# Attention of a head pair: both heads block by block, score products in pieces of 256 columns, value products alternating between the heads

## The reference, cut to what matters

```
p  = x @ w_in                                   # q, k, v of mixers A and B, gates
yA = attention over own chunk (64) + 8 previous chunks, learned relative bias, 16 heads of 64
yB = attention over own chunk + 2 previous chunks, ALiBi bias, sink per head, 16 q heads, 2 kv heads
s  = (q . k) / 8 + bias;  m = max(s) (B: and the sink);  p = exp(s - m)
o  = (p / sum(p)) . v                            # B: sum(p) + exp(sink - m)
h  = LN(alpha x + (sigmoid(gA) (yA wA) + sigmoid(gB) (yB wB)) w_out);  y = LN(alpha h + PEER(h))
```

## Time and profile before

| | |
|---|---|
| median of 3 runs | 4470.74 us |
| span of the profiled execution, first to last instruction | 4456.8 us |
| TensorE busy in the span | 4282.4 us, 96% |
| VectorE, ScalarE, GpSimd busy | 64%, 31%, 60% |
| share of TensorE in the chain that ended last | 66% |
| attention loops | from about 499.5 us to 1317 us of the span |
[...]

### The profile page before, as it was taken

How to read it: one execution, slowest core, us unless ns; L and a number is a source line. 1 busy time by engine, 2 the same in 40 slices (tenths; PEclk the granted TensorE clock), 3 DMA queues, 4 the chain that set the end, 5 groups by cost and what they waited for, 6 DMA issues and landing times.

```text
span 4456.8 us, 71381 instructions
## 1 busy us (share of the span) xinstructions
PE 4282.4 (96%) x26508; PEld 4120.7 (92%) x26508; DVE 2839.1 (64%) x4233; ACT 1376.0 (31%) x2750; POOL 2672.1 (60%) x1665
## 2 busy tenths in 40 slices
PE   8999999999989999799899999999999999999998
PEld 8999888878879999699899999999999999999997
DVE  1000133444442231699997899898997988988988
ACT  1000122222221110311386434343443443443444
POOL 5444322222324545244776778778887888888884
PEclk9999999999999999999999999999999999999999
DMA  5222233222233323112489999999999999999995
GB/s 202 99 102 98 96 119 128 104 81 81 78 119 122 116 90 99 38 66 76 145 276 320 382 376 398 374 372 409 416 405 377 412 418 411 417 411 416 418 418 241
DMA packets 269138, 1083.82 MB, mean 243 GB/s; under 512 B 24560, under 2 KB 90224, under 8 KB 185328
## 3 DMA queue, kind: packets, MB, share of 16 engines
q0 software_dynamic: 74736, 544.24, 29.8%
q1 hardware_dynamic: 89568, 391.16, 23.6%
q10 hardware_dynamic: 104736, 147.39, 9.7%
HBM read 1020.44 MB, written 67.63 MB: 244 GB/s over the span
## 4 chain that ended last, share of the span: by engine, by line
PE 66%; DVE 18%; DMA 6%; issue 5%; POOL 3%; ACT 1%; ACTq 0%; DVEq 0%; POOLq 0%
PE banks L497 30%; PE banks L741 15%; PE banks L675 11%; DVE work L1499 3%; DVE work L1462 2%; DVE banks L1465 2%; POOL w_lo L383 2%; PE banks L729 2%; DMA work<-in_u_rows,idx_all 2%; PE banks L566 2%; PE banks L528 2%; DMA work<-in_v_rows,idx_all 1%; POOL work L411 1%; PE banks L536 1%; DVE work L1371 1%
## 5 line engine op out<-in xcount | busy, mean ns | idle before, releaser
L383 POOL TENSOR_TENSOR w_lo<-w_raw,w_hi 128x1024 fp32r<-128x1024 f32 x472 | 1140.7, 2417 | 243.5 <-ACT w_hi L1057 229.6
L389 POOL TENSOR_SCALAR w_hi<-w_raw 128x2048 fp32r<-128x2048 f32 x134 | 289.6, 2161 | 1326.8 <-PE banks L497 1252.3
L497 PE MATMUL banks<-mv_hi,w_hi 128*128 128x256 f32 x3648 | 863.2, 318 | 62.9 <-DVE mv_lo L1203 35.4
L497 PE MATMUL banks<-mv_lo,w_hi 128*128 128x256 f32 x3648 | 835.8, 310 | 0.0
L497 PE MATMUL banks<-mv_hi,w_lo 128*128 128x256 f32 x3648 | 835.3, 310 | 0.0
L497 PEld LDWEIGHTS banks<-mv_hi,w_hi 128*128 128x128 f32 x3648 | 652.1, 189 | 127.1 <-issue 85.9
L741 PE MATMUL banks<-mv_hi,w_hi 128*128 128x384 f32 x2048 | 693.2, 338 | 43.5 <-ACT part_t L1116 22.1
L393 POOL TENSOR_TENSOR w_lo<-w_raw,w_hi 128x512 fp32r<-128x512 f32 x536 | 721.0, 1377 | 11.2
L675 PE MATMUL banks<-mv_hi,w_hi 128*128 128x384 f32 x2048 | 694.0, 339 | 4.6 <-ACTq L1083 2.0
L741 PE MATMUL banks<-mv_lo,w_hi 128*128 128x384 f32 x2048 | 690.3, 337 | 0.0
L741 PE MATMUL banks<-mv_hi,w_lo 128*128 128x384 f32 x2048 | 690.3, 337 | 0.0
(11 more groups left out here) (166 smaller groups left out, 5319.5 us busy)
## 6 DMA issues: line engine op xcount, KB each, us to landing
w_raw<-in_wstream SPq DMA_DIRECT2D x472, 512.0 KB, 7.9
w_raw<-in_wstream SPq DMA_DIRECT2D x134, 1024.0 KB, 4.8
gate_matrix<-work ACTq DMA_DIRECT2D x12, 2048.0 KB, 9.0
work<-gate_matrix ACTq DMA_DIRECT2D x32, 768.0 KB, 9.0
out_p<-work ACTq DMA_DIRECT2D x34, 320.0 KB, 2.2
work<-out_p ACTq DMA_DIRECT2D x34, 320.0 KB, 3.4
gate_scratch<-work ACTq DMA_DIRECT2D x32, 320.0 KB, 2.2
work<-gate_scratch ACTq DMA_DIRECT2D x16, 640.0 KB, 4.0
```

What stands on the lines that cost most here:

```text
L383: pool.tensor_tensor(w_lo[s][:, part], raw[s][:, part], w_hi[s][:, part].bitcast(f32), ALU.subtract) \
L389: pool.tensor_scalar(w_hi[s][:, :], raw[s][:, :], 1.0, 0.0, ALU.mult, ALU.add).then_inc(hi_done, 1)
L497: last = pe.matmul(acc(dst, h), a[s][:, P * k:P * k + P], b[h][:, k, :], start=(k == k_first and n == 0), stop=(k == k_last and n == 2))
```

## The change

The steps of a pair are reordered: block by block, both heads of a block in one round. `HEADS` becomes (head 0, head 1) of block 0, of block 1, and so on, then the sample; rounds u run over 5 blocks (`NU`) instead of 10 steps. In a round, TensorE computes the scores of both heads (alternating between them, in pieces of at most 256 columns), then k steps, the transposes of the two heads of the block before with k steps between, and the values of both heads of the block two rounds before, alternating between the heads. The buffers for scores, transposed scores, maxima and sums become four (`t % 4`, in `work2` and a wider `small`). VectorE does soft_in of both heads, then soft_out of both heads of the block before, then out_take. Score and output banks stay as they are.

```diff
-        s_sb = [area(5920, 512), area(6432, 512)]
-        pt_sb = [area(6944, 512), area(7456, 512)]
+        s_sb = [area(5920, 512), area(6432, 512), W2[:, 2048:2560], W2[:, 2560:3072]]
+        pt_sb = [area(6944, 512), area(7456, 512), W2[:, 3072:3584], W2[:, 3584:4096]]
...
-        HEADS = [(hh, i) for hh in range(2) for i in range(4)] + [(0, "sample"), (1, "sample")]
+        HEADS = [(hh, i) for i in (0, 1, 2, 3, "sample") for hh in range(2)]
         NS = len(HEADS)
+        NU = NS // 2
...
+            def scores(mix, j, u):
+                i = HEADS[2 * u][1]
+                if u:
+                    pe.wait_ge(s_taken, 1 + STEP_BASE[mix] + NS * j + 2 * u)
...
                 if i == "sample":
                     pe.wait_ge(t_taken, 1 + t_use(mix, j, ("c", 0), 1))
+                    for hh in range(2):
+                        pe.transpose(s_bank[hh][:, 0:P], st_sb[hh][:, :], ident)
+                    at, span, pieces = P, slice(0, P), ((0, P),)
                 else:
+                    w, end = width(mix, i), P * (i + 2)
+                    at, span = 0, slice(end - P, end)
+                    pieces = [(c, min(c + 2 * P, w)) for c in range(0, w, 2 * P)]
+                for lo, hi in pieces:
+                    for hh in range(2):
+                        rows = slice(HD * hh, HD * hh + HD)
+                        first = span.stop - pieces[-1][1] if i != "sample" else 0
+                        last = pe.matmul(s_bank[hh][:, at + lo:at + hi], q_t[rows, span], k_t[rows, first + lo:first + hi],
+                                         start=True, stop=True)
+                        if hi == pieces[-1][1]:
+                            last.then_inc(s_full, 1)
...
+            def values(mix, j, u):
+                i = HEADS[2 * u][1]
+                pe.wait_ge(t_taken, 1 + t_use(mix, j, ("t", 2 * u + 1), 1))
+                pe.wait_ge(o_taken, 1 + STEP_BASE[mix] + NS * j + 2 * u)
...
                     nk = width(mix, i) // P
                     for c in range(nk):
                         kb = i + 2 - nk + c
+                        for o, at, pt in parts:
+                            last = pe.matmul(o, v_nat[:, P * kb + at:P * kb + at + HD], pt[:, P * c:P * c + P],
+                                             start=(c == 0), stop=(c == nk - 1))
+                            if c == nk - 1:
+                                last.then_inc(o_full, 1)
...
-                for t in range(NS + 2):
-                    if t < NS:
-                        scores(mix, j, t)
-                    before = {0: 0, 1: 1, 6: 1, 7: 1} if mix == "a" else {0: 1, 6: 1, 7: 1, NS: 3}
-                    gemm(before.get(t, 2))
-                    if 1 <= t <= NS:
-                        transpose_p(mix, j, t - 1)
-                    if t >= 2:
-                        values(mix, j, t - 2)
-                    if t == 6:
-                        gemm(2)
+                for u in range(NU + 2):
+                    if u < NU:
+                        scores(mix, j, u)
+                    spread = ((1, 0, 0), (2, 1, 1), (1, 1, 1), (1, 1, 1), (1, 1, 1), (2, 1, 0), (2, 0, 0)) if mix == "a" else \
+                        ((2, 0, 0), (2, 1, 1), (1, 1, 1), (1, 1, 1), (2, 1, 1), (2, 1, 1), (2, 0, 0))
+                    early, between, late = spread[u]
+                    gemm(early)
+                    if 1 <= u <= NU:
+                        transpose_p(mix, j, 2 * u - 2)
+                        gemm(between)
+                        transpose_p(mix, j, 2 * u - 1)
+                        gemm(late)
+                    if u >= 2:
+                        values(mix, j, u - 2)
+                    if u == 3:
                         cached_scores(mix, j)
+                gemm(len(k_steps))
...
+                for u in range(NU + 1):
+                    if u < NU:
+                        exponents(2 * u)
+                        exponents(2 * u + 1)
+                    if u:
+                        take(mix, j, ("t", 2 * u - 2))
+                        take(mix, j, ("t", 2 * u - 1))
+                    if u == 3:
                         take(mix, j, ("c", 0))
-                    if t == 6:
                         gate_evacuate(2 * pair, 0, pair)
...
-                    for t in range(NS + 2):
-                        if 1 <= t <= NS:
-                            soft_out(mix, j, t - 1)
-                        if t < NS:
-                            soft_in(mix, j, t)
-                        if t >= 2:
-                            out_take(mix, j, t - 2, j + (PAIRS if mix == "b" else 0))
+                    for u in range(NU + 2):
+                        for t in (2 * u, 2 * u + 1):
+                            if u < NU:
+                                soft_in(mix, j, t)
+                        for t in (2 * u - 2, 2 * u - 1):
+                            if 1 <= u <= NU:
+                                soft_out(mix, j, t)
+                        for t in (2 * u - 4, 2 * u - 3):
+                            if u >= 2:
+                                out_take(mix, j, t, j + (PAIRS if mix == "b" else 0))
```

More of the change, by code:

```diff
@@ L188, in build @@
         mx = [small[:, s:s + 1] for s in range(2)]
-        nmax = [small[:, 2 + s:3 + s] for s in range(2)]
-        rsum = [small[:, 4 + s:5 + s] for s in range(2)]
-        esink = [small[:, 6 + s:7 + s] for s in range(2)]
+        nmax = [small[:, 16 + s:17 + s] for s in range(4)]
+        rsum = [small[:, 20 + s:21 + s] for s in range(4)]
+        esink = [small[:, 24 + s:25 + s] for s in range(4)]
         rden = [small[:, 8 + s:9 + s] for s in range(2)]
@@ L512, in _ @@
                     unit(s, U_QKV + 2 * i + s, (qkv_evac, 2 * i + s + 1), 0)
[L515 to L520, removed]
+            def scores(mix, j, u):
+                i = HEADS[2 * u][1]
+                if u:
+                    pe.wait_ge(s_taken, 1 + STEP_BASE[mix] + NS * j + 2 * u)
+                else:
+                    pe.wait_ge(s_taken, 1 + STEP_BASE[mix] + NS * j)
                 if i == "sample":
                     pe.wait_ge(t_taken, 1 + t_use(mix, j, ("c", 0), 1))
-                    pe.transpose(bank[:, 0:P], st_sb[hh][:, :], ident)
-                    last = pe.matmul(bank[:, P:2 * P], q_t[rows, 0:P], k_t[rows, 0:P], start=True, stop=True)
-                else:
[L526 to L529, removed]
+                    for hh in range(2):
+                        pe.transpose(s_bank[hh][:, 0:P], st_sb[hh][:, :], ident)
+                    at, span, pieces = P, slice(0, P), ((0, P),)
+                else:
+                    w, end = width(mix, i), P * (i + 2)
[9 more added lines that the diff above has]
+                            last.then_inc(s_full, 1)
             def transpose_p(mix, j, t):
@@ L535, in transpose_p @@
                 for c in range(w // P):
-                    last = pe.transpose(t_bank[:, P * c:P * c + P], s_sb[t % 2][:, P * c:P * c + P], ident)
+                    last = pe.transpose(t_bank[:, P * c:P * c + P], s_sb[t % 4][:, P * c:P * c + P], ident)
                 last.then_inc(t_full, 1)
@@ L546, in cached_scores @@
                 last.then_inc(t_full, 1)
[L548 to L553, removed]
+            def values(mix, j, u):
+                i = HEADS[2 * u][1]
+                pe.wait_ge(t_taken, 1 + t_use(mix, j, ("t", 2 * u + 1), 1))
+                pe.wait_ge(o_taken, 1 + STEP_BASE[mix] + NS * j + 2 * u)
+                v_nat = vn if mix == "a" else vn_b
+                parts = [(o_bank[HD * hh:HD * hh + HD, 0:P], HD * hh, pt_sb[(2 * u + hh) % 4]) for hh in range(2)]
                 if i == "sample":
@@ L557, in values @@
                         c = DEC_T * b
[L558 to L561, removed]
+                        for o, at, pt in parts:
+                            pe.matmul(o[:, c:c + DEC_T], cv_t[:, P * b + at:P * b + at + HD],
+                                      pt[:, c:c + DEC_T], start=(b == 0), stop=False)
+                    for o, at, pt in parts:
+                        pe.matmul(o, v_nat[:, at:at + HD], pt[:, P:2 * P], start=False, stop=True).then_inc(o_full, 1)
                 else:
```

50 lines of the change are left out of this document (22 added, 28 removed).

## The result

The changed kernel takes 4518.58 us (median of 4 runs, 4514.69 to 4522.01) against 4470.73 for the kernel before: the ratio is 1.0106, 95% interval 1.0092 to 1.012. It is slower by 48 us; forecast were 69, with a range for the whole of 4510 to 4565 us. The profiled execution has a span of 4520.2 us, 1.8 less than its time of 4522.01; so of the 13.9 us that the prediction puts between span and median before, most is the distance of that execution from the median. The forecast doesn't change by that: it is the median and 69.

What follows compares the result with a forecast made beforehand. TensorE was taken to bound the 16 attention pairs. Eight A pairs at +4.3 us and eight B pairs at +4.7 gave 72, less 3: 69 us over 4470.7, so 4540 us; forecast's own range 4510 to 4565.

Steps and rivals of the forecast that it cites:

- The waits: TensorE at transposes behind both heads' softmax chain: 7.4 us per A pair, 7.35 per B, plus 0.6 for the cached-scores copy.
- the split's inflation: VectorE's normalisation running slower beside GpSimd's split, now on TensorE's path: 0.9 us per B pair.
- The 1.0 us for the split in A pairs: GpSimd's split slowing VectorE's normalisation on TensorE's path in each A pair; bounds 0 and 1.7 us.
- The pairing: Both heads' score and value products partly overlapping on TensorE: 4.4 us saved per A pair, 3.3 per B pair.
- 2n+1 record times instead of 4n: TensorE time for both heads' n products each, near full overlap; 0.1075 us per value block, 0.21 per 256 score columns.
- series: No overlap of the heads' products on TensorE, only entries saved; taken for 128-column scores; as a rival 4568 us, chance 0.13.
- one entry's worth: The sample step on TensorE saves one group entry each for scores and values, 0.36 us per pair together.
- The half of everything: Full overlap, half of all TensorE score and value time saved: 5.75 us per A pair, 4.6 per B; total 4519.
- A rival at 0.05: TensorE's clock falls because of four gaps of 2 to 2.6 us in a pair; chance 0.05.
- the GEMM steps between the gaps: The prediction's argument against TensorE's clock falling: GEMM steps stand between the waits of a pair.
- The 3 us of gain from the later gate evacuation: Two GEMM steps behind the last values delay the second gate evacuation and ScalarE's loads; bounds 0 and 10 us.

Runs made afterwards that it cites:

- e1: The changed kernel with VectorE doing soft_out of block u-1 before soft_in of block u: 4507.64 us, 1.0074 of the kernel before.
- e2: The changed kernel with VectorE's soft_out before soft_in, and ScalarE copying block u-1's transposes in turn with block u's exponentials: 4381.81 us, 0.9796 of the kernel before.
- e8: The changed kernel with a round's GEMM steps ahead of the first transpose in rounds 2 to 4 (in B's round 1, three of four): 4448.37 us, 0.9949 of before.
- e7: The kernel before, without pairing, with VectorE doing soft_in of step t before soft_out of step t-1: 4577.46 us, 1.0232 of the kernel before.
- e5: e2 with the cached products and their copy in round 2, and VectorE taking block u-3's outputs between soft_out and soft_in: 4325.69 us, 0.9683 of before.
- e3_fill: The changed kernel with extra, never read 256-column products put into TensorE's waits ahead of the first transposes: 4481.63 us, 1.0021 of the kernel before.
- e11: e5 with one GEMM step between head 0's and head 1's part of every score and value group: 4494.27 us, 1.0052 of the kernel before.
- e6: e2 with one GEMM step between head 0's and head 1's part of every score and value group: 4537.43 us, 1.014 of the kernel before.
- e10: e5 with whole score products up to 512 columns and head 1's value products behind all of head 0's: 4336.15 us, 0.9712 of the kernel before.

## Why the prediction was right, and where it was not

**The waits: right in place and mechanism, too large in sum.** Forecast 0.47, 2.04, 2.57, 0.62 and 2.34 us in an A pair, found 0.27, 1.88, 2.43, 0.47 and 2.13. In B u=2 and u=3 came as worked out, the split's inflation included (2.01 and 3.09); u=4 gave 0.45 instead of 2.00, because the GEMM steps ahead of it ran at the lower clock: in the two B pairs where they ran at the higher one it is 1.79 and 1.81, in the other six 0.28 to 0.45. The 1.0 us for the split in A pairs was not found: in the pair above the normalisation that it slows is head 1's (1.18 us at 803.04, beside the split from 801.51 to 806.59), and a GEMM step covers that. Idle time grew by 99 us; forecast were 16 pairs of about 8.3, 133. e1, e2 and e8 show that these waits are the order of the lists: changed on VectorE and ScalarE they go, and with the GEMM steps in their place those at the first transposes shrink from 106 to 36 us. e7 shows that the order alone, on the old kernel, is worse than the whole change.

**The pairing: mis-sized by half.** The step "I count a group of n products per head at 2n+1 record times instead of 4n" failed. Both heads take as long as one, 128-column scores (0.42 us, 792.63 to 793.05; one head 0.42, 837.99 to 838.41 before) and the sample's 16-column values too (1.30 us), which the forecast had counted as series or at one entry's worth. The sample's values alone give 1.30 us a pair instead of 0.15. No run shows the 2n+1: in the trace after, the records of both heads' scores of 256 columns start in twos, one of each head, at 794.12 and 794.13 and again at 794.44 and 794.45, and one head's two before start as far apart, at 841.62 and 841.94. The reason given, that the heads share neither rows, columns nor output partitions, holds for neither kind: their score products (64*128 in the rows) share columns and output partitions, their value products (128*64) the rows, and it was enough to be apart in the other (0.63 us for both heads' scores of 256 columns, 1.03 for their values of four blocks). Saved in the loops, at full clock, are 763 - 648 = 115 us, and 763 - 640 = 123 in e5, where 62 were forecast. The half of everything, the prediction's other end, is the better estimate of this term, 83; it leaves the sample's products out as well. That it gives 4519 for the whole is chance, since it leaves out the clock.

**The clock: a rival at 0.05 that came true in part.** It takes 58 us more than before: 31 stretches at the lower level in the loops, 140 us together, against one of 10 us before. One fall as the earlier trace rows show it, 3 us at 0.50, loses 1.5 us, and three in each of the 16 pairs would lose 72, near the 58; the chance given to it was not. The argument against it, the GEMM steps between the gaps, does not hold: e3_fill shows that the gaps matter (0.98 instead of 0.92 when they are filled), and e11 that listed gaps aren't needed (0.93 in the 50 us from 710, with TensorE listed busy for 49.62).

**The sum.** +99 for idle time, -115 for the pairing and +58 for the clock are the 43 us of the loops, to 1 us. The forecast of +69 was made of +130 and -62, with nothing for the clock. So the waits were 31 us too large, and the pairing 53 too small, which the 58 of the clock covered. That the sum was near is in good part luck: with the pairing sized rightly and the clock still left out, the same working gives about 15 us more than before instead of 69, and with the measured waits too 16 less. The 3 us of gain from the later gate evacuation no run shows; they are less than the spread of the part behind the loops.

## What to carry to other kernels

When steps are merged into pairs, write down for every engine what now stands between the end of a product and the operation that hands it back: what was one head's chain became two, and with VectorE's list alone reordered (e1) TensorE's waits for its normalisation went from 106.4 us to 13.0, while 75.9 for ScalarE's copies came in their place. Put the instruction that releases the bounding engine first on every list that it passes through; changed on one list alone (e1) it gained 11 us, on both 137. The two heads' products, on disjoint halves of the array, gained by being neighbours: a GEMM step between them cost some 125 us (e6, e11), giving up the alternation about 6 (e10).

## What the runs showed of the hardware

- fp32 products of two heads on rows 0 to 63 and 64 to 127, or with outputs on columns 0 to 63 and 64 to 127, take as long as those of one head: 0.63 us for 256 columns (one head 0.63), 1.03 for four blocks (1.01), 1.30 for the sample's values (1.30).
- This holds for products that stand head behind head in the list, up to two blocks per head (0.67 us against 0.66); with three and four the overlap is partial (1.07 against 0.80 to the start of the next row, and 1.58 against 1.09 to the end of the last).
- With a GEMM step between the heads there is none: each head takes its own 1.13 us for 512 columns (e6, 800.05 and 802.19), where both together took 1.14.
- The granted clock went down to the lower level in the change, where TensorE waits for about 2 to 3 us in several rounds of each pair (31 stretches in the loops), behind single waits of 5.14 us (before) and 3.52 us (e5, its only fall), and also in a window where TensorE was listed busy for 49.62 of 50 us (e11, behind sixteen records of 32 columns).
- A normalisation of 128 x 256 on VectorE took 1.12 us and an addition of 128 x 1 took 1.24 while GpSimd worked on the split (1077.04 to 1082.05), 0.35 and 0.15 otherwise.
